# A middle norm summed with GpSimd's help, a router taken by quarters of the rows, a dense pass written out, and expert loads issued at the merge

## The chip, the cores and the metric

One NeuronCore of a Trainium2 chip runs the whole program. The time is device microseconds (us) of one execution; the median of several is given. Engines: TensorE (PE in the profile, PEld its weight loads), VectorE (DVE), ScalarE (ACT), GpSimd (POOL) and SyncE (SP), which here only issues DMAs.

## The reference

The program is a two-layer encoder trunk on 256 tokens of 1024 float32 channels. Per layer:

```
h = rmsnorm(x, g_mix[l]);  p = h @ w_in[l]
merged = gated sum of three branches (FoX attention, sparse attention, RWKV-7)
x = x + merged @ w_out[l]
h = rmsnorm(x, g_ffn[l])                      # the middle norm
layer 0: x = x + (silu(h @ w_gate) * (h @ w_up)) @ w_down          # d_ff 2816
layer 1: logits = h @ router_w + router_b; top 2 of 8, softmax -> gates
         x = x + sum_e gates[e] * swiglu_e(h)                      # d_ff 3584
out = rmsnorm(x, g_final)
```

rmsnorm is `x * rsqrt(mean(x*x) + 1e-6) * g` over the 1024 channels of a token.

## The kernel before, in words

Channels lie on partitions: x and h are [128, 8, 256], eight slices k of 128 channels by 256 tokens. Everything is float32; the profile records each full matmul as two. Each engine has its own instruction stream, written out by hand in program order, and waits on named semaphores (`need`, `wait_ge`). `open_bank`/`close_bank` take the 8 PSUM banks in turn on TensorE, `take`/`done` read and release one on another engine, `need_sb` waits until a bank has been read out.

**Weights.** SP issues all loads in program order. The mixers and the dense pass stream weights through three 2 MB slots in turn; the memory of slots 3 to 7 holds the mixer's tensors meanwhile (gates among them). The expert stage uses all eight as a ring, load n in slot n modulo 8, each load waiting for `slots_used`. A slot's next load waits for the bank that its last user closed (`before`, `released`). Ahead of the dense loop (L1211 to L1216) SP waits for all three slots, then issues gate, up and down loads; ahead of the experts it waits until all four output products have been added to x (L1241).

**End of a mixer (L847 to L877).** TensorE computes `pr0..3` (L856); VectorE multiplies by the gates and adds (L2000 to L2006, semaphore `merged`, 4 a layer). Then four output products `xo0..3` (L869), each 16 matmuls of 256 columns. VectorE adds each to x (L2010), ScalarE squares that pair of slices (L1414, `squares`), TensorE sums the squares over partitions with a matrix of ones, two matmuls a pair (L371), a pair behind each later product and the last after the fourth. ScalarE loads the table of the square root (L1416), takes it (L1426); VectorE takes the reciprocal (L1668) and makes the eight slices of h (L1671, `h_ready`).

**Dense pass (L888 to L923).** Five passes of 512 hidden channels run in a hardware loop and a last one of 256 follows: 32 gate matmuls, 32 up matmuls, 32 down matmuls per pass (L385, L909), the down products accumulating in banks 4 to 7. Four matmuls with zeros (L918) start these banks ahead of the loop, so that the loop never has to; TensorE then waits for all of h.

**Router (L932 to L967).** TensorE waits for all of h, makes the logits of each 128 tokens with 8 matmuls of 8 columns and one for the bias (L938, L939), then 16 transposes of h (L948) that ScalarE evacuates to ht, tokens on partitions. VectorE finds the top two (L2040 to L2060), ScalarE exponentiates (L1605), TensorE counts tokens per expert (L953 to L957) and spreads the table of items (L961, L962), VectorE makes the one-hot selections (L2110 to L2128). Then the first gather (L984) collects an item's tokens.

**Expert loop (L1004 to L1084).** One turn per item of up to 96 tokens: gate and up (L1030), down (L1047), the next gather, and the scatter of the item before (L994). It runs eight turns here.

GpSimd builds masks at the start, makes `Lo` (L1376) and copies in the mixer, and after layer 1 clears Ys and SpT (L1391 to L1394).

## Time and profile before

| | us |
|---|---|
| median of three runs | 1888.19 |
| lowest, highest | 1883.44, 1894.51 |
| the profiled execution | 1888.6 |
| its span in the trace | 1886.9 |
| busy: TensorE / VectorE / ScalarE / GpSimd | 1811.0 / 392.7 / 234.1 / 44.6 |

The span runs from the first instruction to the last in the trace; the execution's own time is 1.7 us longer. "Chain" below is the chain of work that ended last, followed back from the end: at each step to what released it. A piece "x64" of full matmuls is 32 of them. A window gives engine busy times, the clock granted to TensorE as a share of full speed, the share of time that the DMA engines were busy, and GB/s.

### The profile page before, as it was taken

Reading aid. Unit: us, or ns where it says so; the run is one execution under the profiler, and the core shown is the slowest. Engines: PE = TensorE matmul, PEld = TensorE weight load, DVE = VectorE, ACT = ScalarE, POOL = GpSimd, SP = SyncE. Lnnn points to the kernel's source line nnn. Section 1 sums busy time; section 2 is a strip of 40 time slices with the busy share of each in tenths; the row PEclk is TensorE's granted clock in tenths of the full one; section 3 lists DMA queues with packets and bytes.
Section 4 is the critical chain, followed back from the end, with each engine's and each line's share of the span. In section 5 each row is a group of like instructions: output and inputs, shape, how many; then the busy total and the mean of one; then the engine's idle time right before and its main releaser. Section 6 shows DMA issues by size and latency. Waiting matters only on the chain.

```text
span 1886.9 us, 42790 instructions
## 1 busy us (share of the span) xinstructions
PE 1811.0 (96%) x19764; PEld 1165.7 (62%) x19764; DVE 392.7 (21%) x807; ACT 234.1 (12%) x460; POOL 44.6 (2%) x102
## 2 busy tenths in 40 slices
PE   6999999999999999999799999999999999999996
PEld 5787878788887778878535444353443534445344
DVE  1256233100001456133310101101010010101102
ACT  1324120100001324111100000000000000000001
POOL 3000200000000000100000000000000000000000
PEclk9999999999999999989799999999999999999998
DMA  6432212543434332212899999999999999999970
GB/s 189 156 134 90 92 52 84 190 166 133 174 102 140 112 134 90 92 46 90 334 342 375 393 383 401 372 381 389 370 415 370 386 376 378 414 378 383 369 294 24
DMA packets 122842, 462.13 MB, mean 245 GB/s; under 512 B 9567, under 2 KB 20497, under 8 KB 106289
## 3 DMA queue, kind: packets, MB, share of 16 engines
q1 hardware_dynamic: 122672, 459.46, 64.0%
q8 instruction: 157, 2.57, 0.5%
q14 instruction: 13, 0.10, 0.0%
HBM read 458.39 MB, written 1.05 MB: 243 GB/s over the span
## 4 chain that ended last, share of the span: by engine, by line
PE 95%; DVE 2%; ACT 1%; issue 1%; SPq 0%; DMA 0%; DVEq 0%; ACTq 0%
PE bank L1030 31%; PE bank L385 26%; PE bank L1047 15%; PE bank L909 4%; PE bank L869 3%; PE bank L730 2%; PE bank L856 1%; PE bank L984 1%; PE bank L994 1%; PE bank L692 1%; PE bank L424 1%; PE bank L371 1%; PE bank L379 1%; PE bank L783 0%; PE bank L661 0%
## 5 line engine op out<-in xcount | busy, mean ns | idle before, releaser
L1030 PE MATMUL bank<-slot,xg 128*32 128x512 f32 (+1 forms) x6144 | 581.9, 539 | 0.0
L385 PE MATMUL bank<-h,slot 128*128 128x256 f32 x2176 | 488.0, 384 | 8.0 <-ACT rel L1478 5.3
L385 PEld LDWEIGHTS bank<-h,slot 128*128 128x128 f32 x2176 | 415.1, 192 | 70.5 <-issue 14.2
L1030 PEld LDWEIGHTS bank<-slot,xg 128*32 128x32 f32 x6144 | 198.9, 110 | 372.3 <-issue 369.0
L1047 PE MATMUL bank<-slot,aT 128*32 128x256 f32 x5376 | 293.0, 379 | 0.0
L1047 PEld LDWEIGHTS bank<-slot,aT 128*32 128x32 f32 x5376 | 174.9, 110 | 118.6 <-issue 6.2
L2154 DVE TENSOR_TENSOR av<-gs,bank 128x512 f32<-128x512 f32 (+1 forms) x48 | 29.8, 622 | 577.0 <-PE bank L1030 575.0
L909 PE MATMUL bank<-hid,slot 128*128 128x256 f32 x352 | 77.0, 380 | 0.9 <-DVE hid L2022 0.9
L909 PEld LDWEIGHTS bank<-hid,slot 128*128 128x128 f32 x352 | 66.9, 190 | 10.2 <-issue 1.2
L1622 ACT ACTIVATE gs<-bank 128x512 f32<-128x512 f32 (+1 forms) x48 | 25.2, 543 | 284.6 <-PE bank L1030 284.5
L869 PE MATMUL bank<-sq,slot 128*128 128x256 f32 x256 | 56.2, 379 | 0.0
L1627 ACT ACTIVATE SpT<-bank 128x512 f32<-128x512 f32 x8 | 4.8, 597 | 413.8 <-PE bank L1077 413.8
L869 PEld LDWEIGHTS bank<-sq,slot 128*128 128x128 f32 x256 | 48.7, 190 | 6.6
L2022 DVE TENSOR_TENSOR hid<-hsig,bank 128x512 f32<-128x512 f32 x11 | 7.6, 688 | 216.5 <-PE bank L385 216.5
L2142 DVE TENSOR_TENSOR x<-x,bank 128x512 f32<-128x512 f32 x36 | 22.4, 683 | 102.3 <-PE bank L994 102.3
L2170 DVE STREAM_TRANSPOSE xg<-bank 128x256 f32<-128x256 f32 x24 | 10.8, 450 | 136.0 <-PE bank L984 136.0
L1376 POOL TENSOR_TENSOR Lo<-Bm,level 128x512 f32<-128x512 f32 x16 | 21.1, 1334 | 722.4 <-DVE Bm L1893 678.9
L1507 ACT ACTIVATE gates<-bank,VB 128x256 f32<-128x256 f32 x48 | 20.1, 469 | 128.2 <-PE bank L385 128.1
L1622 ACT ACT_TABLE_LOAD x8 | 10.3, 1283 | 186.6 <-PE bank L1030 186.6
L984 PE MATMUL bank<-ht,Sl 128*32 128x256 f32 x432 | 26.9, 400 | 5.0 <-DVE Sl L2128 5.0
L2157 DVE STREAM_TRANSPOSE aT<-av 128x512 f32<-128x512 f32 (+1 forms) x48 | 30.9, 645 | 1.6
L994 PE MATMUL bank<-SpT,Ys 32*128 32x256 f32 x432 | 26.5, 383 | 1.8 <-DVE Ys L2172 1.0
(407 smaller groups left out, 1086.9 us busy)
## 6 DMA issues: line engine op xcount, KB each, us to landing
slot<-in_moe_w_gate SPq DMA_DIRECT2D x32, 2048.0 KB, 12.5
slot<-in_moe_w_up SPq DMA_DIRECT2D x32, 2048.0 KB, 17.9
slot<-in_moe_w_down SPq DMA_DIRECT2D x32, 2048.0 KB, 10.5
slot<-in_moe_w_gate SPq DMA_DIRECT2D x32, 1536.0 KB, 9.0
slot<-in_moe_w_up SPq DMA_DIRECT2D x32, 1536.0 KB, 11.1
slot<-in_moe_w_down SPq DMA_DIRECT2D x32, 1536.0 KB, 8.8
slot<-in_w_in SPq DMA_DIRECT2D x20, 2048.0 KB, 8.1
slot<-in_ffn_w_gate SPq DMA_DIRECT2D x5, 2048.0 KB, 7.8
```

The lines of the kernel that those rows point to most:

```text
L385: ins = mm(o, w[:, k, c:c + n], rhs[:, k, :], start=k == 0, stop=k == nk - 1)
L730: ins = mm(b[:, j, :], w[:, off + k, m * P:(m + 1) * P], src[:, k, :], start=k == 0, stop=k == nk - 1)
L869: ins = mm(b[:, j, :], w[:, k, 256 * g + P * j:256 * g + P * j + P], sq[:, k, :], start=k == 0, stop=k == KD - 1)
L909: ins = mm(v2(banks[4 + m // 2])[:, m % 2, :], w[:, k, m * P:(m + 1) * P], hid[:, k, :], start=first and k == 0, stop=last and k == nf - 1 ...
L984: ins = mm(banks[g][32 * p:32 * p + 32, 0:256].rearrange("s (b c) -> s b c", c=32), Sl[:, tt, 32 * g:32 * g + 32], strip(ht[:, tt, :], p), ...
L994: ins = mm(v2(banks[SCAT[p]])[:, j, :], Ys[32 * p:32 * p + 32, g, j * P:(j + 1) * P], SpT[32 * p:32 * p + 32, g, :], start=g == 0, stop=g ...
L1030: ins = mm(o.rearrange("s (b c) -> s b c", c=32), xg[:, g, k, :], strip(w[:, kk, :], p), start=k == 0, stop=k == KD - 1)
L1047: ins = mm(o[32 * p:32 * p + 32, :], aT[:, g, nb_ * q + b, :], w[:, b, 256 * p:256 * p + 256], start=half == 0 and q == 0 and b == 0 and g ...
L1622: A(gs[:, g, 0:width], banks[g][:, 0:width], ACT.Silu).then_inc(S["gs_done"], 1)
L2142: tt_(o, o, v2(banks[SCAT[p]]), ALU.add).then_inc(S["x_done"], 1)
L2154: tt_(av[:, g, 0:width], gs[:, g, 0:width], banks[3 + g][:, 0:width], ALU.mult).then_inc(S["av_done"], 1)
L2157: V.transpose(aT[:, g, 0:width // 32, :].rearrange("p b c -> p (b c)"), av[:, g, 0:width]).then_inc(S["aT_done"], 1)
```

## The change

Seven edits:

- *Sums.* In both layers GpSimd adds the squares of slices 2, 3 and then 4, 5 to those of slices 0, 1 (`added`). In layer 0 TensorE sums only slices 0, 1 and 6, 7, all after the fourth product.
- *Router by quarters (layer 1).* After each addition to x, VectorE multiplies two slices by the norm's weight alone into h (`xw_ready`). TensorE makes the logits and transposes of quarters 0 and 1 behind output products 1 and 2, and 2 and 3 behind the last. The sums of squares come out per token, in two columns of the logits' bank, from matmuls with one column of ones. ScalarE takes the root (`std_tok`), VectorE the reciprocal (`rs_tok`); the logits are scaled with it and the bias added on VectorE, and ht is scaled where ScalarE evacuates it.
- *Bias.* `b_rt` is loaded to 128 partitions.
- *First dense pass written out.* It starts banks 4 to 7 itself, and its first 8 matmuls wait slice by slice for h; the loop has four turns left. The zero matmuls are gone.
- *Dense loads.* Each of the first three waits for its own slot alone.
- *Expert loads.* The ring begins at slot 3 (`ring_at`). Loads 0 to 4 wait for layer 1's last `merged`, load 5 and later for the four additions to x, as before.
- A last wait for h counts one norm less, since layer 1's middle norm no longer makes h.

The diff, with unchanged lines and the list of semaphore names cut:

```diff
@@ -129,7 +129,8 @@
         w_rt = place("w_rt", [P, KD, NE])
-        b_rt = place("b_rt", [1, NE])
+        b_rt = place("b_rt", [P, NE])
+        rst = place("rst", [P, NT])
         x = place("x", [P, KD, T])
@@ -316,6 +317,9 @@
             released[name] = (bank_full[b], n)
+        def ring_at(n):
+            return (n + NS) % NSE
@@ -857,6 +861,37 @@
                 ssn = 2 * l + 1
+                tok = {}
+                def sums(ks):
+                    for tt in range(NT):
+                        for k in ks:
+                            ins = mm(tok["rt"][:, 2 * NE + tt:2 * NE + tt + 1], nsqs[1][:, k, tt * P:(tt + 1) * P],
+                                     ones[:, 0:1], start=False, stop=False, skip_group_check=True)
+                    return ins
+                def routed(g):
+                    need(pe, "xw_ready", g + 1)
+                    if g == 0:
+                        tok["rt"] = open_bank(pe, "rt")
+                    if g % 2 == 0:
+                        for tt in range(NT):
+                            tok[tt] = v4(open_bank(pe, f"ht{tt}{g // 2}"))
+                    ks = range(2 * g, 2 * g + 2)
+                    for tt in range(NT):
+                        for k in ks:
+                            mm(tok["rt"][:, tt * NE:(tt + 1) * NE], h[:, k, tt * P:(tt + 1) * P], w_rt[:, k, :],
+                               start=g == 0 and tt == 0 and k == 0, stop=False, skip_group_check=True)
+                    if g == 3:
+                        need(pe, "squares", 4 * ssn + g + 1)
+                        close_bank(sums(ks), "rt")
+                    for tt in range(NT):
+                        for k in ks:
+                            ins = nc.tensor.transpose(tok[tt][:, k % 4, :], h[:, k, tt * P:(tt + 1) * P], ident[:, :])
+                        if g % 2:
+                            close_bank(ins, f"ht{tt}{g // 2}")
                 for s in range(2):
@@ -869,12 +904,23 @@
                         close_bank(ins, n)
-                        if s == 0 and g == 1:
-                            ssb = open_bank(pe, f"ss{ssn}")
-                        if s or g:
-                            squares(ssb, ssn, 2 * s + g - 1, nsqs[l])
+                        if l and (s or g) and s + g < 2:
+                            routed(2 * s + g - 1)
                     free_slot(f"{l}wo{s}", f"{l}xo{2 * s + 1}")
-                close_bank(squares(ssb, ssn, 3, nsqs[l]), f"ss{ssn}")
+                if l:
+                    routed(2)
+                    need(pe, "added", 4)
+                    sums(range(2))
+                    routed(3)
+                else:
+                    b = open_bank(pe, f"ss{ssn}")
+                    need(pe, "added", 2 * (l + 1))
+                    for k in range(2):
+                        mm(b[:, 0:T], ones[:, :], nsqs[l][:, k, :], start=k == 0, stop=False)
+                    need(pe, "squares", 4 * ssn + 4)
+                    for k in range(KD - 2, KD):
+                        ins = mm(b[:, 0:T], ones[:, :], nsqs[l][:, k, :], start=False, stop=k == KD - 1)
+                    close_bank(ins, f"ss{ssn}")
@@ -897,7 +943,12 @@
                                 b = v2(banks[bi])
-                                unit(b[:, 0, :], w, 256 * g, P)
+                                if first and bi == 0:
+                                    for k in range(KD):
+                                        need(pe, "h_ready", KD + k + 1)
+                                        mm(b[:, 0, :], w[:, k, 0:P], h[:, k, :], start=k == 0, stop=k == KD - 1)
+                                else:
+                                    unit(b[:, 0, :], w, 256 * g, P)
                                 unit(b[:, 1, :], w, 256 * g + P, P).then_inc(bank_full[bi], 1)
@@ -907,18 +958,17 @@
                                     ins = mm(v2(banks[4 + m // 2])[:, m % 2, :], w[:, k, m * P:(m + 1) * P],
-                                             hid[:, k, :], start=first and k == 0, stop=last and k == nf - 1,
+                                             hid[:, k, :], start=first and k == 0 and m % 2 == 0, stop=last and k == nf - 1,
                                              skip_group_check=True)
...
                                     ins.then_inc(S["down_part"], 1)
+                                if first and g == 0 and m % 2:
+                                    ins.then_inc(bank_full[4 + m // 2], 1)
                         ins.then_inc(S["down_done"], 1)
-                    for bi in range(4, 8):
-                        mm(banks[bi][:, :], cst[:, 0:1].broadcast_to([P, P]), cst[:, 0:1].broadcast_to([P, 512]),
-                           start=True, stop=False, skip_group_check=True).then_inc(bank_full[bi], 1)
-                    need(pe, "h_ready", KD * 2)
-                    with pe.Fori(0, DI) as i:
+                    dense(0, 4, True, False)
+                    with pe.Fori(1, DI) as i:
                         dense(i, 4, False, False)
@@ -928,25 +978,6 @@
-            l = 1
-            need(pe, "h_ready", KD * 4)
-            b = open_bank(pe, "rt")
-            br = b[:, 0:2 * NE].rearrange("p (t e) -> p t e", t=2)
-            for tt in range(NT):
-                for k in range(KD):
-                    mm(br[:, tt, :], h[:, k, tt * P:(tt + 1) * P], w_rt[:, k, :], start=k == 0, stop=False)
-                ins = mm(br[:, tt, :], ones[0:1, :], b_rt[:, :], start=False, stop=True)
-            close_bank(ins, "rt")
-            for tt in range(NT):
-                for g in range(2):
-                    n = f"ht{tt}{g}"
-                    b = v4(open_bank(pe, n))
-                    for j in range(4):
-                        k = 4 * g + j
-                        ins = nc.tensor.transpose(b[:, j, :], h[:, k, tt * P:(tt + 1) * P], ident[:, :])
-                    close_bank(ins, n)
@@ -1005,7 +1036,7 @@
                 def slot(n):
-                    si, r = n % NSE, n // NSE
+                    si, r = ring_at(n), n // NSE
                     pe.wait_ge(slot_full[si], i * 48 + 16 * (loads[si] + r + 1))
@@ -1094,7 +1125,7 @@
             ins.then_inc(S["y_item"], 1)
-            need(pe, "h_ready", KD * (n + 1))
+            need(pe, "h_ready", KD * n)
             for tt in range(NT):
@@ -1129,7 +1160,7 @@
             vec(1, 48, lk(a["vres_v0"]))
-            sp.dma_start(b_rt[:, :], a["router_b"]).then_inc(S["rows_in"], 16)
+            sp.dma_start(b_rt[:, :], a["router_b"].broadcast_to([P, NE])).then_inc(S["rows_in"], 16)
@@ -1211,13 +1242,16 @@
                     sl3 = [(st0 + s) % NS for s in range(3)]
-                    for si in sl3:
-                        sm, v = before[(si, ld[si])]
-                        sp.wait_ge(sm, v)
                     wg = a["ffn_w_gate"][0].rearrange("(k p) n -> p k n", p=P)
...
                     wd = a["ffn_w_down"][0].rearrange("(k p) n -> p k n", p=P)
-                    with sp.Fori(0, DI) as i:
+                    for si, t_, src in ((0, c3(slots[sl3[0]], KD, 512), wg[:, :, 0:512]),
+                                        (1, c3(slots[sl3[1]], KD, 512), wu[:, :, 0:512]),
+                                        (2, c3(slots[sl3[2]], 4, D), wd[:, 0:4, :])):
+                        sm, v = before[(sl3[si], ld[sl3[si]])]
+                        sp.wait_ge(sm, v)
+                        sp.dma_start(t_, src).then_inc(slot_full[sl3[si]], 16)
+                    with sp.Fori(1, DI) as i:
                         srcs = [wg[:, :, bass.ds(i * 512, 512)], wu[:, :, bass.ds(i * 512, 512)],
@@ -1238,8 +1272,6 @@
-            for g in range(4):
-                need_sb(sp, f"1xo{g}")
             mg = a["moe_w_gate"][0].rearrange("e (k p) n -> e p k n", p=P)
@@ -1253,15 +1285,20 @@
                             src = t_[bass.ds(e, 1), :, r0:r0 + nb_, :]
-                            dst = c3(slots[n % NSE], nb_, D)
+                            dst = c3(slots[ring_at(n)], nb_, D)
                         else:
                             src = t_[bass.ds(e, 1), :, 2 * q:2 * q + 2, c0:c0 + 4 * width]
-                            dst = c3(slots[n % NSE], 2, 4 * width)
+                            dst = c3(slots[ring_at(n)], 2, 4 * width)
                         free(n)
-                        sp.dma_start(dst, src.rearrange("o p k n -> (o p) k n")).then_inc(slot_full[n % NSE], 16)
+                        sp.dma_start(dst, src.rearrange("o p k n -> (o p) k n")).then_inc(slot_full[ring_at(n)], 16)
                         n += 1
+            need(sp, "merged", 8)
             def first_free(n):
+                if n == NSE - NS:
+                    for g in range(4):
+                        need_sb(sp, f"1xo{g}")
                 if n >= NSE:
@@ -1387,6 +1424,15 @@
                                           Tt[o, :, :]).then_inc(S["t_copied"], 1)
+                o = nsqs[l]
+                for g in range(1, 3):
+                    need(gp, "squares", 4 * (2 * l + 1) + g + 1)
+                    if g > 1:
+                        need(gp, "added", 2 * l + 1)
+                    nc.gpsimd.tensor_tensor(o[:, 0:2, :], o[:, 0:2, :], o[:, 2 * g:2 * g + 2, :],
+                                            ALU.add).then_inc(S["added"], 1)
+                need(gp, "added", 2 * l + 2)
@@ -1587,8 +1633,8 @@
                 norm_sq(2 * l + 1, nsqs[l], x_out)
-                norm_std(2 * l + 1)
                 if l == 0:
+                    norm_std(2 * l + 1)
                     fl, _, _ = loop_fill["d"]
@@ -1600,13 +1646,16 @@
+            b = take(act, "rt")
+            A(rst[:, :], b[:, 2 * NE:2 * NE + NT], ACT.Sqrt, bias=cst[:, 1:2]).then_inc(S["std_tok"], 1)
             need(act, "route", 1)
+            need(act, "rs_tok", 1)
             for tt in range(NT):
...
                 for g in range(2):
-                    evac(f"ht{tt}{g}", ht[:, tt, 512 * g:512 * g + 512])
+                    evac(f"ht{tt}{g}", ht[:, tt, 512 * g:512 * g + 512], scale=rst[:, tt:tt + 1])
             act.wait_ge(S["tab_ready"], 2)
@@ -2008,11 +2057,18 @@
                     done(tt_(o, o, b, ALU.add), f"{l}xo{g}")
+                    if l:
+                        need_sb(dve, f"{l}xo{g}")
+                        for k in range(2 * g, 2 * g + 2):
+                            ins = V.tensor_scalar(h[:, k, :], x[:, k, :], col(VA, 24 + k), None, ALU.mult)
+                            if k % 2 == 0:
+                                step(ins)
+                        ins.then_inc(S["xw_ready"], 1)
                 for g in range(4):
...
                 V.memset(cst[:, 6:7], 0.0).then_inc(S["x_ready"], 1)
-                norm(2 * l + 1, 16 + 8 * l)
                 if l == 0:
+                    norm(2 * l + 1, 16 + 8 * l)
                     fl, _, _ = loop_fill["d"]
@@ -2036,9 +2092,18 @@
+            need(dve, "std_tok", 1)
+            V.reciprocal(rst[:, :], rst[:, :]).then_inc(S["rs_tok"], 1)
+            need(dve, "rs_tok", 1)
             b = take(dve, "rt")
-            done(V.tensor_copy(lg[:, :, :], b[:, 0:2 * NE].rearrange("p (t e) -> p t e", t=2)), "rt")
+            for t in range(NT):
+                ins = V.scalar_tensor_tensor(out=lg[:, t, :], in0=b[:, t * NE:(t + 1) * NE], scalar=rst[:, t:t + 1],
+                                             in1=b_rt[:, :], op0=ALU.mult, op1=ALU.add)
+                if t == 0:
+                    step(ins)
+            done(ins, "rt")
             need_sb(dve, "rt")
+            sync()
             for t in range(NT):
...
             sync()
```

## Rows read from the trace of the kernel before

**Rows 1.** the page, part 1: busy time, share of the span, instructions

```profile
PE 1811.0 (96%) x19764; PEld 1165.7 (62%) x19764; DVE 392.7 (21%) x807; ACT 234.1 (12%) x460; POOL 44.6 (2%) x102
```

**Rows 2.** expert turn: us, busy PE, PEld, DVE, ACT, POOL, clock, DMA share, GB/s

```profile
1163.00:1278.00 115.00, 115.00 (x1554) 51.25 (x1546) 13.27 (x24) 5.80 (x10) 0.00 (x0) 1.00 0.98 384
```

**Rows 3.** the chain in order of time, end of layer 0's mixer (start, us, what)

```profile
320.26 0.86 PE bank L371 x4
...
328.03 0.86 PE bank L371 x4
...
337.21 1.25 ACT L1416
...
339.10 1.76 DVE rs L1668
```

**Rows 4.** the same chain, end of layer 1's mixer to the expert loop

```profile
887.88 0.86 PE bank L371 x4
...
896.51 6.92 PE bank L869 x32
...
911.81 3.58 PE bank L938 x16
...
919.95 3.29 PE bank L948 x16
...
923.36 0.22 PE bank L954 x2
...
924.29 0.17 DVE pos L2074
...
932.93 4.50 PE bank L984 x48
```

**Rows 5.** groups by line and shape, GpSimd and VectorE (busy us, mean ns | idle)

```profile
L1376 POOL TENSOR_TENSOR Lo<-Bm,level 128x512 f32<-128x512 f32 x16 | 21.1, 1334 | 722.4 <-DVE Bm L1893 678.9 <-PE bank L692 43.5
...
L1714 DVE TENSOR_SCALAR F<-F 128x256 f32<-128x256 f32 x2 | 0.6, 285 | 0.0
```

**Rows 6.** the chain over the whole span, its longest pieces

```profile
344.50 29.58 PE bank L385 x128
...
387.89 27.63 PE bank L385 x128
...
579.47 1.76 DVE rs L1668
581.89 5.16 PE bank L379 x16
...
787.20 1.51 issue
```

**Rows 7.** the timeline at both middle norms (start, us, engine, line, operation)

```profile
336.24 0.40 SPq L1225 DMA_DIRECT2D slot<-in_ffn_w_gate  x1
...
338.21 3.61 PE L918 MATMUL bank<-cst 128*128 128x512 f32 x8
...
904.23 2.09 SPq L1261 DMA_DIRECT2D slot<-in_moe_w_gate  x4
...
920.20 0.24 DVE L2043 MAX8 mr<-lg 128x8 f32<-128x8 f32 x2
...
922.17 0.18 DVE L2060 TENSOR_TENSOR sl<-sl,eqr 128x16 f32<-128x16 f32 x1
```

**Rows 8.** the page, part 6: DMA issues, us from issue to landing

```profile
slot<-in_ffn_w_gate SPq DMA_DIRECT2D x5, 2048.0 KB, 7.8
```

**Rows 9.** the same view and columns, router and transposes of layer 1

```profile
912.00:924.00 12.00, 12.00 (x61) 11.90 (x62) 2.84 (x19) 2.71 (x6) 0.00 (x0) 0.55 1.02 426
```

**Rows 10.** the timeline at the start

```profile
6.37 0.25 SPq L1132 DMA_DIRECT2D b_rt<-in_router_b  x1
...
8.31 0.45 PE L348 MATMUL bank<-ident,rows 126*128 126x126 f32 x1 [8.31 <-DMA b_rt<-in_router_b]
```

**Rows 11.** DMA issues in the first 40 us

```profile
xt<-in_x SPq DMA_DIRECT2D x1, 1024.0 KB, 5.1
```

More of the change, by code:

```diff
@@ L234, in trunk @@
             "consts", "rows_in", "x_in", "smallw_in", "vecs", "sq_ready", "std_ready", "h_ready",
-            "x_ready", "squares", "fox_z", "fox_e", "fox_l", "fox_F", "max_ready", "exp_ready", "p_ready",
+            "x_ready", "squares", "added", "fox_z", "fox_e", "fox_l", "fox_F", "max_ready", "exp_ready", "p_ready",
             "css", "cstd", "cn_ready", "sel_ready", "shift_ready", "k_ready", "tanh_ready", "masks", "amasks", "w_zero",
@@ L239, in trunk @@
             "rel_used", "hid_sig", "hid_ready", "gates_in", "hT_done", "route", "route_e", "route_x",
-            "route_g", "route_n", "route_c", "route_t", "sel_item",
+            "route_g", "route_n", "xw_ready", "std_tok", "rs_tok", "route_c", "route_t", "sel_item",
             "out_tok", "stored", "vector_step", "scalar_step", "pool_step",
```

## The prediction

> **What bounds the kernel now.** I read the page first. Its busy line [rows 1] gives TensorE 1811.0 of 1886.9 us, so a gain has to shorten TensorE's work or one of the few stretches in which it waits. The windows view settles the second half of the kernel: in one turn of the expert loop [rows 2] TensorE is busy 115.00 of 115.00 us at granted clock 1.00, the DMA engines are busy 0.98 of the time and move 384 GB/s. TensorE sets the pace there and the loads just keep up. So whatever lets the expert loop begin earlier moves the end one to one. The chain of waits, read around the two middle norms, shows where TensorE is not in control. After layer 0's mixer [rows 3] it goes from TensorE's sums through ScalarE's table load and VectorE's reciprocal, and the dense pass starts at 344.50. After layer 1's mixer [rows 4] it runs from 903.43 (the last output product's end, 896.51 + 6.92) to the first gather at 932.93: 29.5 us of norm, router and routing chain. The change edits exactly these two places.
>
> **Layer 0, sums of squares.** Before, each pair of squares is summed by two matmuls behind the next output product; a pair takes 0.86 us [rows 3]. Two pairs lie between output products (320.26 and a like one at 328.03), on the chain. GpSimd now folds pairs 1 and 2 into pair 0 and four matmuls are left, all after the last product. That takes 2 x 0.86 = 1.7 us off the chain. The adds cost nothing if GpSimd keeps up: a 128x512 two-input operation takes it 1334 ns [rows 5], and its second add can start when the third squares exist, some 1.4 us after the third product, with 6.9 us of the fourth product over it; then TensorE needs it. Without that cover each would cost its 1.3 us. Behind the last product the chain stays: squares, ScalarE's table load of 1.25 us at 337.21, root, reciprocal 1.76 us from 339.10 [rows 3]; TensorE's first two remaining matmuls fit in front of the last squares, and the other two, 0.86 us, end under the table load.
>
> **Layer 0, start of the dense pass.** From the reciprocal's end at 340.86 to the end of the first 64 matmuls (344.50 + 29.58 = 374.08 [rows 6]) it was 33.2 us. Two things held it: all eight slices of h, and the gate weights, whose load was issued at 336.24 [rows 7] and takes 7.8 us to land [rows 8], so 344.0. Now each of the three loads waits for its own slot, and the gate load goes out when the branch weights are free, some 28 us earlier: it is covered. Matmul k waits for slice k alone. The kernel does this already at layer 1's first product [rows 6]: reciprocal ends 579.47 + 1.76 = 581.23, the eight gated matmuls (two records each) start at 581.89 and take 5.16, not the 3.45 us of eight at full clock (27.63/64 = 0.432 each), so the clock dip is in it. By that pattern: 0.66 + 5.16 + 56 x 0.432 = 30.0 us, a gain of 3.2. The old first batch has its dip too: 29.58 against 27.63 for 64 matmuls. The four zeroing matmuls (0.59 us records from 338.21 [rows 7]) lay under VectorE's work and cost nothing; without them TensorE idles some 3.5 us before h instead of 2.7, after which the rows show a dip anyway. Bounds: no dip, 1.7 more; twice the old dip, 1.9 less. The Trainium skill (TensorE: Matmul & The Clock Gate, "The HAM clock gate") has it that the half clock is what an idle array returns to and that activity releases it, which speaks against taking the zeroing away; by it alone this gain would be about 1.3. The trace agrees so far as that a batch after 2.7 us of idling took 29.58 us, not 27.63. The written-out pass adds no work; its first down matmuls start the banks themselves. Layer 0 together: **4.9 us** (3.0 to 6.6).
>
> **Layer 1, router.** A quarter of the router is 4 matmuls of 8 columns and 4 transposes. At half clock the 8 matmuls from 911.81 took 3.58 us and the 16 transposes from 919.95 took 3.29 [rows 4], the clock being 0.55 in that stretch [rows 9]; at full clock I take half, 0.22 and 0.10 to 0.12 (the full-clock pair at 923.36 took 0.22 [rows 4]). So a quarter is 0.88 + 0.48 = 1.36 us. After the second output product (887.88 [rows 4]): quarter 0, product 6.91, quarter 1, product 6.92: the last product ends at 904.43, 1.0 later than before (two quarters in, two pairs of sums out). Then quarter 2 (1.36), four one-column sums (0.88), quarter 3's router (0.88), four more sums (0.88): logits closed at 908.4. The last slice comes in time: VectorE's add 0.70 and two scalings at 0.29 each [rows 5] end 1.3 us after the product, the last squares 1.4 after, both before TensorE's 2.2 us are over. The first three quarters' scalings lie under output products. GpSimd's second add is some 5 us early here too. Before, VectorE copied the logits in 0.2 us and began the maxima at 920.20 [rows 7]. Now a small root (about 0.2), reciprocal and two scale-and-adds of small tiles (0.17 and 0.36) stand between, so maxima begin at 909.3. Exp's table load (1.3 us, like the other) moves behind that root and ends about 910.0; exp is wanted some 2 us after the maxima, so it stays hidden, as do the four evacuations of h's transpose, done by 913. From 920.20 to the gather at 932.93 were 12.7 us. In them TensorE was still transposing until 923.24 although sl was ready at 922.35 (922.17 + 0.18) [rows 7]: 0.9 goes. But the five count matmuls from 923.24 ran in a short full-clock spell (1.05 us to 924.29 [rows 4]); with nothing before them they would run at half clock, 1.1 more. So the gather starts at 909.3 + 12.9 = 922.2 to 922.4: **10.5 us** earlier (8.5 to 11.6: the lower end has TensorE at half clock for about half of its 4 us of small matmuls, the upper one the count matmuls at full clock).
>
> **Early expert loads.** Five go out at the last merge, near 875.5, instead of 904.23 [rows 7]. Nothing is queued on SP behind the new wait but these loads; w_out's landed long before. I cost this at nothing, neither gain nor loss: TensorE never waited for an expert load, and at 426 GB/s [rows 9] a 2 MB load takes 4.9 us, so five have landed by 901 and three more, issued near 905, by 920, before the gather is done. Were the loads needed, the new start would have been the first to feel it.
>
> **Start.** The router bias goes to 128 partitions instead of one, and it is the last of the small loads that TensorE's first transpose waits for: issued at 6.37, released 8.31 [rows 10]. Bounds: nothing, and 3.2 us (the 1 MB load of x takes 5.1 to land [rows 11] against these 1.9). It is 4 KB, so near the low end: **0.7 us lost**, on the path.
>
> **Sum.** 4.9 + 10.5 - 0.7 = 14.7. The profiled execution is 1888.6 us (span 1886.9), 0.4 over the median of 1888.19; so 1888.2 - 14.7 = **1873.5**. About 0.5%, 9.4 us, is what a measurement of this kernel can tell from no change.
>
> **Rivals.** (a) *The clock takes the gain.* The small matmuls behind the last product (4.0 us) run wholly at half clock, +4.0; the quarter between products brings a dip like the old one, +1.9; the dense start a longer one, +1.7. Gain 7.1: 1881. For: TensorE was at half clock through 11 us of just such matmuls [rows 9]. Against: before these it had stood idle 6 us; now it comes from full-size products. Chance 0.14, three parts of it within 0.5%. (b) *The token-side chain is longer than I count* (root, reciprocal, bias, exp's table on the path, about 3 us, and the bias load at its bound, 2.5 more): gain 9.2: 1879. Chance 0.08, half within 0.5%. (c) *TensorE waits for instructions at loop turns*, and it is slower. Both loops sit at other places in a longer stream; the row at 787.20 [rows 6] is such a gap, 1.51 us with nothing to wait for. Place: the four dense and eight expert turns, the latter with the DMA engines full. It decides from 1.2 us a turn (12 turns against 14.7); at 1.5 times the row, 2.25 each, it is 27 us: 1900. Against: TensorE is busy 115.00 us of 115.00 over a stretch that holds a turn's end [rows 2]. The Trainium skill (Runtime: NRT & Kernel Launch, "Instruction fetch mechanics") says that a taken branch outside the blocks at hand has to fetch its target before going on; the trace of before shows no such wait at that turn. Chance 0.04. (d) *It does not do what it says*: the first two quarters are not fed in time and TensorE waits the 1.3 us from a product's end to its scaled slice at each of three quarters, 3.9 in all: gain 10.8, 1877. Each slice has a whole product, 6.9 us, over it; this is inside the forecast's range and chance.
>
> **Numbers.** My forecast has 0.74, nearly all above 0.5%. Faster 0.80, same 0.16, slower 0.04. The terms' bounds give gains of 8.3 to 18.2, so 1870 to 1880; the runs of before scatter from 1883.44 to 1894.51, so I add about 3 each side: 1867 to 1883. That takes in (a), (b), (d) and leaves out (c).
>
> **What would show it.** Right: the third and fourth output products of layer 0 back to back; dense start near 340 with eight matmuls in about 5 us; gather about 18 us after layer 1's last product, not 29.5; GpSimd's adds done several us before TensorE's sums; expert turns still without idle. Wrong: TensorE waiting on GpSimd or on scaled h, a half-clock stretch that begins before the last product ends, gaps at loop turns, the first transpose later than 10 us, or any wait for an expert slot.

## The result and the profile after

The changed kernel takes 1938.8 us (median of 4, 1934.88 to 1945.04) against 1886.53 (1883.44 to 1894.51): ratio 1.0278, 95% interval 1.025 to 1.0306. It is 2.8% slower. 1873.5 was predicted, in a range of 1867 to 1883. Time in brackets is the lowest and highest run, or behind a ratio its 95% interval; every run below was measured beside the kernel before, whose median was 1883.7 to 1887.2 in those batches.

The changed kernel's page, part 1 (busy time) and the shares of the chain:

```profile
PE 1823.3 (94%) x19744; PEld 1160.6 (60%) x19744; DVE 390.2 (20%) x808; ACT 234.2 (12%) x460; POOL 49.7 (3%) x106
...
PE 93%; issue 3%; DVE 2%; ACT 1%; SPq 0%; DMA 0%; DVEq 0%; ACTq 0%
```

TensorE's busy time rose by 12 us [rows 1] and its share of the longer span fell; 3% of the chain is "issue", time in which the engine waits for nothing that the profile shows. The waits of TensorE, longest in total first (us in total, times, longest):

```profile
PE bank L1061 <- issue: 44.2, 14, 5.1
PE bank L352 <- DMA b_rt<-in_router_b: 9.2, 1, 9.2
PE bank L696 <- issue: 6.1, 6, 1.6
```

Before, L1061 (then L1030, the expert loop's gate and up products) had no such wait at all; now it has 14, two for each of seven returns to the loop's head. The chain at layer 0, behind layer 1's mixer, and around the first two returns (start, us, what):

```profile
308.93 27.64 PE bank L904 x128
...
342.28 6.42 PE bank L949 x16
348.70 24.17 PE bank L389 x112
...
386.68 27.63 PE bank L389 x128
...
872.14 13.81 PE bank L904 x64
...
920.64 4.75 PE bank L1015 x48
925.39 10.30 PE bank L1061 x96
...
1037.56 2.77 PE bank L1015 x48
1040.81 4.54 issue
1045.36 4.47 PE bank L1061 x17
1050.63 10.61 PE bank L1061 x79
...
1163.11 2.77 PE bank L1015 x48
1166.36 4.59 issue
1170.95 3.74 PE bank L1061 x17
1174.69 1.53 issue
```

The first turn, entered from above, is as before: 10.30 us for the 96 matmul records of L1061 behind the gather at 920.64. The second, whose gather starts at 1037.56, begins with 4.54 us of nothing, then 17 records in 4.47 us, another gap of 0.8 (1.53 at the next return), then the other 79 records. The busy view by stretch shows the rest of the cost (us, busy PE, PEld, DVE, ACT, POOL, clock, DMA share, GB/s):

```profile
1041.00:1045.00 4.00, 0.00 (x0) 0.00 (x0) 0.11 (x1) 0.00 (x0) 0.00 (x0) 0.89 1.01 412
1045.00:1049.00 4.00, 3.65 (x17) 0.97 (x18) 0.00 (x0) 0.00 (x0) 0.00 (x0) 0.50 1.02 420
1049.00:1052.00 3.00, 2.20 (x9) 0.43 (x11) 0.00 (x0) 0.00 (x0) 0.00 (x0) 0.50 0.99 404
```

The idle stretch is followed by half clock (0.50; still 0.50 from 1052 to 1054, then 0.91 from 1054 to 1056), at which the first records of the turn run. From gather to gather (1037.56 to 1163.11) a turn is 125.55 us here. Over the seven turns that begin with a return the mean is 124.77 against 114.93 before: 7 x 9.84 = 68.9 us lost. The first gather itself comes at 920.64 instead of 932.93 [rows 4]: 12.3 us gained. The difference, 56.6, is the difference of the two spans to 0.2 us (1943.3 and 1886.9). (Up to the loop a single trace can't tell the gain closely: in the seven traces whose code ahead of the loop is the same, this one among them, the first gather starts between 913.42 and 922.00, while the piece from layer 1's first output product to the gather is 48.5 in six of them and 49.3 in one.) So most of what the change was costed for happened (12.3 of 14.7 us), and something else took more than five times as much.

At layer 0 the output products now start at 308.93 and all four run back to back in one piece of 27.64 us. The eight gated matmuls (342.28) take 6.42 us. From the first output product to the end of the dense pass's first 64 matmuls it is 348.70 + 24.17 - 308.93 = 63.9 us, against 67.6 before (306.45 to 374.08, the end in [rows 6]). Behind layer 1's last product, which ends at 902.34, in the timeline's order (start, us, engine, line):

```profile
895.61 1.27 POOL L1433 TENSOR_TENSOR nsq<-nsq 128x512 f32<-128x512 f32 x1 [6.92 <-ACT nsq L1460]
...
902.18 0.95 PE L884 MATMUL bank<-w_rt,h 128*128 128x8 f32 x8
...
903.10 0.62 DVE L2063 TENSOR_SCALAR h<-x,VA 128x256 f32<-128x256 f32 x2
...
903.46 0.95 PE L869 MATMUL bank<-ones,nsq 128*128 128x1 f32 x8
...
904.27 1.04 PE L884 MATMUL bank<-w_rt,h 128*128 128x8 f32 x8
...
907.12 0.24 DVE L2108 MAX8 mr<-lg 128x8 f32<-128x8 f32 x2
...
909.32 0.59 PE L984 MATMUL bank<-sl,upto 128*128 128x8 f32 x2 [2.63 <-DVE sl L2125]
...
911.66 0.17 DVE L2139 TENSOR_TENSOR pos<-bank,sl 128x16 f32<-128x16 f32 x1 [1.57 <-PE bank L988]
```

GpSimd's second add is done at 896.9, 6.6 us before TensorE's sums (L869) read it at 903.46. The last scaled slices (L2063) are there at 903.7, before the last router matmuls at 904.27. The maxima (L2108) begin 4.8 us after the last product, not 16.8.

### The profile page after: what moved, and what is told of

Its sections match the earlier page's. It is cut to its first block, busy times and chain, and to the rows that moved or that the text cites. A ratio compares the mean times of both kernels' runs of the same rounds, so it can differ in the third digit from the quotient of the medians.

```text
span 1943.3 us, 42748 instructions
## 1 busy us (share of the span) xinstructions
PE 1823.3 (94%) x19744; PEld 1160.6 (60%) x19744; DVE 390.2 (20%) x808; ACT 234.2 (12%) x460; POOL 49.7 (3%) x106
## 4 chain that ended last, share of the span: by engine, by line
PE 93%; issue 3%; DVE 2%; ACT 1%; SPq 0%; DMA 0%; DVEq 0%; ACTq 0%
PE bank L1061 31%; PE bank L389 25%; PE bank L1078 15%; PE bank L960 4%; PE bank L904 3%; PE bank L734 2%; PE bank L860 1%; PE bank L1015 1%; PE bank L1025 1%; PE bank L696 1%; PE bank L428 1%; PE bank L383 1%; PE bank L375 0%; PE bank L787 0%; PE bank L665 0%
## 5 line engine op out<-in xcount | busy, mean ns | idle before, releaser
L1061 PE MATMUL bank<-slot,xg 128*32 128x512 f32 (+1 forms) x6144 | 605.5, 552 | 44.2 <-issue 44.2
L389 PE MATMUL bank<-h,slot 128*128 128x256 f32 x2160 | 481.5, 382 | 5.3 <-ACT rel L1524 5.3
L1061 PEld LDWEIGHTS bank<-slot,xg 128*32 128x32 f32 x6144 | 204.2, 112 | 435.8 <-issue 434.3
L389 PEld LDWEIGHTS bank<-h,slot 128*128 128x128 f32 x2160 | 409.6, 191 | 68.1 <-issue 12.5
L960 PEld LDWEIGHTS bank<-hid,slot 128*128 128x128 f32 x352 | 66.8, 190 | 10.3 <-issue 1.2
L904 PEld LDWEIGHTS bank<-sq,slot 128*128 128x128 f32 x256 | 48.5, 190 | 6.5
L1671 ACT ACT_TABLE_LOAD x8 | 10.3, 1283 | 256.4 <-PE bank L1061 256.4
L860 PE MATMUL bank<-yT,slot 128*128 128x256 f32 x128 | 28.0, 379 | 0.0
```

The source lines that it names most:

```text
L389: ins = mm(o, w[:, k, c:c + n], rhs[:, k, :], start=k == 0, stop=k == nk - 1)
L860: ins = mm(b[:, j, :], w[:, k, m * P:(m + 1) * P], yT[:, k, :], start=k == 0, stop=k == 3)
L904: ins = mm(b[:, j, :], w[:, k, 256 * g + P * j:256 * g + P * j + P], sq[:, k, :], start=k == 0, stop=k == KD - 1)
L960: ins = mm(v2(banks[4 + m // 2])[:, m % 2, :], w[:, k, m * P:(m + 1) * P], hid[:, k, :], start=first and k == 0 and m % 2 == 0, stop=last ...
L1061: ins = mm(o.rearrange("s (b c) -> s b c", c=32), xg[:, g, k, :], strip(w[:, kk, :], p), start=k == 0, stop=k == KD - 1)
L1671: A(gs[:, g, 0:width], banks[g][:, 0:width], ACT.Silu).then_inc(S["gs_done"], 1)
```

## The experiments

**Placing the loop of the changed kernel.**

```diff
+            pe.addr_align(256, offset=125, max_nops=0)
             pe.br("item_loop")
```

> The kernel after, with one edit: the first instruction of TensorE's expert loop is placed at position 125 of a block of 256 instructions (my estimate of where it lies in the kernel before; in the changed kernel everything ahead of it has moved it on by 92 positions). If the place of the loop in the instruction stream makes the waits of 4.5 and 1.6 us at each turn (theory 1), they go: no idle at the turns, a turn of 114.9 us, the gather still at 920.6, the whole near 1873 us. If the early expert loads or a full load queue make them (theory 2), they stay: about 1939 us. If position 125 is not what before had but the theory holds, the waits change in length.

Measured: 1871.71 us (1867.03 to 1873.53), ratio to before 0.9931 (0.9909 to 0.9954). No wait at any return; the chain, second turn:

```profile
917.55 4.92 PE bank L1015 x48
...
1034.63 2.73 PE bank L1015 x48
1037.36 10.30 PE bank L1062 x96
```

The turn is 114.89 us and the 96 records take 10.30 again. One instruction that computes nothing is worth 67 us. Theory 1 is right for this kernel, and the DMA engines are as busy at this return (1.00 to 1.02 from 1036 to 1042) as at the bad one.

**The mirror: the kernel before, placed at 217** (same line, offset 217).

> The kernel before, with one edit: its expert loop's first instruction placed at position 217, my estimate of where the changed kernel has it. Theory 1 (place): each of seven returns to the loop's head costs 9 to 10 us more, so 1886.5 + 7 x 9.7 = about 1954 us. Theory 2 (early loads): nothing changes, 1886.5 us.

Measured: 1917.09 us (1914.31 to 1922.6), ratio 1.0178 (1.015 to 1.0206). An untouched kernel loses 33 us by place alone, about half of the 67 that I expected. The likely reason is that my estimate of the changed kernel's position was off by an instruction or two; no run places it at 218 to 220, so that is not shown. The second turn:

```profile
1052.24 2.55 PE bank L1031 x18
1054.79 2.41 issue
1057.20 8.78 PE bank L1031 x78
```

There is no wait at the branch, only the inner one, 2.41 us after 18 records. 18 matmuls with their weight loads are 36 instructions, and 256 - 217 = 39: TensorE runs to the end of the block that holds the loop's head and waits for the next. At 217 the branch is at the very end of its block (217 + 38 = 255); in the changed kernel, whose inner wait comes one record earlier, it would lie just behind a block's start (the wait after 17 records puts the head at 218 to 220).

**No early expert loads, nothing placed** (the ring begins at slot 0; all expert loads wait for the additions).

```diff
-            return (n + NS) % NSE
+            return n % NSE
-            need(sp, "merged", 8)
+            for g in range(4):
+                need_sb(sp, f"1xo{g}")
```

> The kernel after without its early expert loads: the ring begins at slot 0 again and all expert loads wait for layer 1's four additions. TensorE's stream has the same instructions at the same places. Theory 1 (place): the waits at the turns stay, within 1 us of 1939, which also tests my nothing for the early loads. Theory 2 (early loads): the waits go, 1873 us.

Measured: 1944.59 us (two runs), ratio 1.0324 (1.0292 to 1.0355), mean turn 125.2 us. The early loads don't make the waits. It is 5.8 us more than the changed kernel's 1938.8, where within 1 was expected, with intervals that overlap; two runs can't tell whether that is real, and the placed pair below shows no difference.

**The prefetch hint 144 instructions earlier** (`if q == 1` for `if q == 2` at the mark).

> The kernel after with TensorE's prefetch hint for the branch back 144 instructions earlier in the loop body, 399 ahead of the branch instead of 255. If the distance of the hint is what matters (theory 3), the 4.5 us wait at each turn goes, and perhaps the 1.6 us one, 1873 to 1895 us. If it is the place of the loop's branch and head in their blocks (theory 1), both waits stay and the time is 1939 us.

Measured: 1940.31 us, ratio 1.0301 (1.0278 to 1.0323), 14 waits of 45.0 us in all. The distance between hint and branch is not what counts. Theory 3 falls.

**Control: the kernel before placed at 125.**

> Control: the kernel before with its expert loop's head placed at position 125 too. If the place theory is right and before already lay in a harmless place, the same as before, 1884 us within 3, no wait at the turns. If placing alone made the other kernel faster, this one is faster than before by some us as well, and the gain of the edits is smaller by that.

Measured: 1886.47 us (10 runs) against 1885.68 (18 runs), ratio 1.001 (0.9995 to 1.0025), mean turn 114.95. Placing is worth nothing where the place was harmless, so the gain of the placed changed kernel belongs to the edits: 12.0 us by the medians beside each other (1883.71 and 1871.71), 13 by the ratio.

**Placed at 125, without the early loads.**

> The placed kernel (expert loop at 125) without its early expert loads. My prediction costs them at nothing: 1871.7 us within 2. A rival: the loads keep the first expert turn fed only because they start early, so 1875 to 1880 and TensorE idle at its first expert products.

Measured: 1871.16 us (1869.84 to 1872.32), ratio 0.993 (0.9909 to 0.9952), against 1871.71 with them. They are worth nothing that these runs can tell, as costed.

**The dense part as before, nothing placed.** The loop takes all passes again, with the zeroing matmuls, the wait for all of h and the old load order; router, sums and expert loads stay as changed.

```diff
-                    dense(0, 4, True, False)
-                    with pe.Fori(1, DI) as i:
+                    for bi in range(4, 8):
+                        mm(banks[bi][:, :], cst[:, 0:1].broadcast_to([P, P]), cst[:, 0:1].broadcast_to([P, 512]),
+                           start=True, stop=False, skip_group_check=True).then_inc(bank_full[bi], 1)
+                    need(pe, "h_ready", KD * 2)
+                    with pe.Fori(0, DI) as i:
```

> The kernel after with layer 0's dense part as before (all passes in the loop, four zeroing matmuls, a wait for all of h, loads behind three waits) and nothing placed. The expert loop's head then lies 115 positions earlier than in the changed kernel, near position 103 by my estimate. Place theory: no waits at the turns, 1871.7 plus the dense start's gain (3 us predicted; 2 by the two traces) = 1874 us. If something else in the changed kernel makes the waits (router quarters, GpSimd's adds, early loads), they stay: 1940 us.

Measured: 1872.62 us (1869.98 to 1878.2), ratio 0.9938 (0.992 to 0.9956). Taking one harmless pass out of the stream takes 66 us away without any alignment: the loop's head moves to 371 instructions earlier. A turn is 115.21 us, 0.3 more than the shortest, and TensorE's waits at L1057 are two, of 0.6 us in all. The chain at its dense pass:

```profile
307.79 27.64 PE bank L904 x128
...
344.11 27.89 PE bank L389 x128
372.00 13.81 PE bank L955 x64
```

From the first output product to the end of the first 64 matmuls it is 64.2 us, only 0.3 more than the 63.9 of the changed kernel (62.6 to 64.2 over the nine versions with the written-out pass and no zeroing): here the first batch runs at full clock (27.89 for 64), where the kernel before had 29.58 [rows 6].

**Placed at 230.**

> The kernel after with the expert loop's head at position 230: 26 instructions before a block boundary, and its branch back 13 instructions behind one. Place theory: the wait inside the loop's top comes after about 11 matmul records instead of 17 and is longer than 2.4 us, some 3 us; the wait at the branch shortens only a little from 4.5 us, since 13 instructions are about 1 us. Turn about 124 us, the whole 1930 to 1945 us. If the wait at the branch needs the branch right at the boundary, it is gone: about 1905 us.

Measured: 1944.83 us, ratio 1.0322 (1.0282 to 1.0362), mean turn 125.2. The second turn:

```profile
1033.28 2.77 PE bank L1015 x48
1036.54 3.63 issue
1040.17 3.39 PE bank L1062 x12
1043.55 2.14 issue
```

Both waits, the inner one after 12 records (24 instructions; 256 - 230 = 26).

**Placed at 190 and at 30.**

> The kernel after with the expert loop's head at 190: 66 instructions ahead of a block boundary, its branch back at 228. By the place theory, in its finer form: the block behind the loop's head arrives some 4.8 us after the head runs (2.6 us of work and 2.0 to 2.4 of waiting at head 217). 66 instructions are about 3.5 us, so a wait of 1.3 us at each turn; no wait at the branch, which is 228 instructions into its block: 1871.7 + 7 x 1.4 = 1881 us. If any place away from the exact boundary is free of waits, 1872.

> The kernel after with the expert loop's head at 30, its branch back then 68 instructions into a block. By the finer form: the branch's target is fetched only once TensorE is in the branch's block, and takes about 5 us; 68 instructions of the gather are 1.9 us, so 3 us of waiting at the branch, with a half-clock start behind it, and no wait at the head: 1895 to 1905 us. If only a branch in the first few instructions of a block waits, 1872.

Measured at 190: 1887.75 us (8 runs), ratio 1.0022 (1.0008 to 1.0036), mean turn 116.93. At 30: 1892.91 us (1892.71 to 1894.67), ratio 1.0048 (1.003 to 1.0066), mean turn 117.63. The returns:

```profile
1033.28 3.43 PE bank L1062 x31
1036.71 1.54 issue
1038.25 7.46 PE bank L1062 x65
```

```profile
1038.01 2.77 PE bank L1015 x48
1041.26 1.62 issue
1042.88 10.51 PE bank L1062 x96
```

At 190 only the inner wait is left, 1.54 us after 31 records (62 instructions of 66). At 30 only the one at the branch, 1.62 us in the chain (2.15 us of idling), shorter than the 3 expected. At 190, 1881 was expected, 1887.75 came, since a turn is 2.0 us longer and not 1.4, and TensorE waits once more behind the last turn (2.30 us ahead of L1025; 1.89 at 217 ahead of L994). At 30 a half-clock start was expected and none came: the clock stays at 1.00 behind these short waits, at 30, 190 and 217 alike. Together with 217 the sizes fit one account. The next block is there 4.97 us after the loop's head runs (3.43 + 1.54) at 190, and 4.96 (2.55 + 2.41) at 217: a fetch of about 5 us. The loop's head is there 4.1 us after TensorE has run into the branch's block at 30 (68 instructions of the gather, 1.9 us, + 2.15), about 4.5 at 230, and 5.0 in the changed kernel, where the branch would be the block's first or second instruction. At 125 both fetches are covered by work.

**Placed at 125, the hint taken out.**

```diff
-                    if q == 2:
-                        near_end = pe.mark_branch_hint_location()
-                pe.br_lt(item_reg, items, on_true="item_loop", on_false="item_end").branch_hint(near_end)
+                pe.br_lt(item_reg, items, on_true="item_loop", on_false="item_end")
```

> The placed kernel (expert loop at 125) with TensorE's prefetch hint for the branch taken out. If the hint is what brings the loop's head in at a good place, TensorE now waits at each of the seven turns about as it did at a bad place, 4 to 5 us plus a half-clock start, also at position 125: 1871.7 + 7 x 6 = 1915 us. If the hint does nothing and only the place counts, 1872 us.

Measured: 1931.99 us (1927.87 to 1933.31), ratio 1.0242 (1.0215 to 1.0269), mean turn 122.9. The second turn:

```profile
1039.07 2.77 PE bank L1015 x48
1042.33 4.46 issue
1046.79 13.37 PE bank L1062 x96
```

Without the hint the return waits 4.46 us at a good place too, and the 96 records take 13.37 us instead of 10.30, about 29 of them at half clock (3.07 us more at 0.107 each). That is 60 us in all, more than the 43 expected, because the half-clock start costs 3 us of each turn's 8. The hint works, if the branch lies far enough inside its block.

**The fetches themselves.** The DMA view has a row for the fetching of instructions (packets, MB, share of the DMA engines' time). In the changed kernel's page, and then for the idle stretch alone, 1040.4 to 1045.3:

```profile
q8 instruction: 164, 2.69, 0.6%
```

```profile
q8 instruction: 1, 0.02, 1.3%
```

A packet is 16.4 KB. Narrower windows place this one: it moves from 1042.50 to 1043.5, and there is no other from 1040.4 to 1048.2; the next moves from 1048.29, in front of the inner wait's end. The same reading for the second turn of each run, in us from the start of its gather (whose last matmul ends at 2.8):

| run | packet starts | wait ends |
|---|---|---|
| changed kernel, return | 4.94 | 7.80 |
| changed kernel, inner | 10.73 | 13.07 |
| 230, return | 4.07 | 6.89 |
| 230, inner | 10.05 | 12.41 |
| 30, return | 2.10 | 4.87 |
| 125 without hint, return | 4.97 | 7.72 |
| 190, inner | 5.14 | 7.69 |
| 217 (kernel before), inner | 5.07 | 7.69 |

Each of the eight waits ends 2.3 to 2.9 us after such a packet starts. At 125 with the hint a packet starts at -0.73 and the next at 5.09, and nothing waits. In the changed kernel the return's packet starts when it does without any hint (4.94 and 4.97, 2.2 us behind the gather): the hint gained nothing there. At 30 and 230 it starts 1.3 and 1.7 us after TensorE has run into the branch's block. So the waits are waits for instructions. That the hinted fetch begins only once TensorE is in the branch's block fits these four starts; it is a reading, since the packets don't say which block they carry.

**Placed at 125, with zeroing ahead of the written-out pass, and the bias loaded late.** Four matmuls with zeros stand in front of the dense pass again, and the bias is the last of the later small loads.

```diff
+                    for bi in range(4, 8):
+                        mm(banks[bi][:, :], cst[:, 0:1].broadcast_to([P, P]), cst[:, 0:1].broadcast_to([P, 512]),
+                           start=True, stop=False, skip_group_check=True)
                     dense(0, 4, True, False)
```

> The placed kernel (expert loop at 125) with two repairs. First, four matmuls with zeros stand again ahead of layer 0's written-out dense pass. If the clock falls there because TensorE idles longer than before (the eight gated matmuls took 5.4 to 6.7 us, 5.2 expected), they take about 4 us now, 2 us gained; if the dip has nothing to do with the zeroing, they stay at 5.4 to 6.7. Second, the bias load goes to the end of the small loads, so TensorE's first transpose starts at 8.3 again or earlier, not 9.2: 0.9 us gained. Together 1871.7 - 2.9 = 1869 us; without the clock effect 1871.

Measured: 1867.49 us (1863.55 to 1875.72), ratio 0.9916 (0.9895 to 0.9937): the fastest median of all, though its interval overlaps that of the placed kernel without them. The trace shows both parts. The start of TensorE's transposes of x (L362) and the dense pass:

```profile
9.11 3.62 PE bank L362 x16
...
337.39 3.69 PE bank L971 x8
341.07 3.45 PE bank L949 x16
344.53 24.17 PE bank L389 x112
```

The eight gated matmuls (341.07) take 3.45 us instead of 5.11 to 6.66 in the nine other versions with a written-out pass. The granted clock is 1.00 from 334 to 344.5 here; in the changed kernel it was 0.74 from 340 to 342, TensorE idle, and 0.50 from 342 to 347. The dip is the price of taking the zeroing away. But the zeroing (3.69 us from 337.39) now ends 34.7 us after the first output product starts, and without it the gated matmuls start 33.35 after (342.28 - 308.93), so 1.3 of the 1.7 to 3.2 us is given back. TensorE's transposes of x start at 9.11 instead of 9.92.

## Why the prediction was wrong

**The step that failed is rival (c).** I named its mechanism, place and row, and then gave it 0.04, priced at 2.25 us a turn, because "TensorE is busy 115.00 us of 115.00 over a stretch that holds a turn's end" [rows 2]. That row says that the loop's old place was harmless. It says nothing of the new place, and the change moves the loop by 92 positions. So the sum held nothing for waits for instructions, and the rival's price was too small by a factor of four: 9.84 us at each of seven returns, 68.9 in all. The 1.51 us gap [rows 6] that I priced by is one wait in straight code; a return at a bad place has two waits, 4.5 and 0.8 to 1.8, and the first brings half clock to the products behind it. The dense loop's three returns (the prediction counts twelve turns, which hold ten returns) cost nothing: the chain has its batches of 27.63 us at 428.12, 469.56 and 511.00 with no wait in front of them. The Trainium skill (Runtime: NRT & Kernel Launch, "Instruction fetch mechanics") has blocks of 256 instructions and a fetch at a taken branch whose target is not at hand. I wrote that the trace of before shows no such wait, and let a fact of one place speak against a rule about places. The runs agree with the rule, and with its 256: the inner wait stands at 24, 36 and 62 recorded instructions behind heads at 230, 217 and 190, where 26, 39 and 66 are left of a block. Of the positions tried 103 (estimated) to 125 were free or nearly so, and 30, 190, 217 and 230 cost 2 to 10 us a turn. They were chosen, not drawn, so they don't give the chance that would have been right; with nothing known of the position 0.04 was too low.

**Without it the sum held.** Placed, the changed kernel gains 12 to 13 us; 14.7 was the forecast. Its 1871.7 us is nearer to the 1873.5 forecast than that partly by luck: the kernel before took 1883.7 beside it, not the 1888.2 that the sum starts from.

- *Sums and start of the dense pass:* 4.9 predicted, 3.7 measured (63.9 against 67.6 us; 3.4 to 5.0 over the nine versions). The first part, two pairs of sums off the chain, came as costed; a kernel with it and the old dense pass has 64.2 us. The written-out pass adds 0.3 us (0 to 1.6 over the versions) instead of 3.2, because I sized its eight gated matmuls by the ones at layer 1 (5.16) and they took 6.42 (5.11 to 6.66 over the versions), and the old first batch's dip, 1.95 us in [rows 6], is gone without the written-out pass too, once the sums are out of the way (27.89). I had costed the zeroing matmuls at nothing and they were worth 1.7 to 3.2 us of clock, though 1.3 of it goes to their own length. The rule that the prediction quotes from the Trainium skill (TensorE: Matmul & The Clock Gate, "The HAM clock gate"), that half clock is what an idle array returns to, was nearer than my row: by it this gain was 1.3, and 2.0 was measured (3.7 less the 1.7 of the sums). The same eight matmuls behind zeroing take 3.45.
- *Router:* 10.5 predicted, 10.4 measured: 872.14 to 920.64 is 48.5 us, against 58.9 before (874.06 to 932.93). Its parts agree: router matmuls near full clock (0.95 and 1.04 us for four; eight took 3.58 before [rows 4]), the count matmuls at half clock from 909.32 to 911.66 (2.3 us, 2.2 predicted), transposes no longer in front of them.
- *GpSimd's adds and early loads:* nothing predicted, nothing measured.
- *Bias:* 0.7 lost predicted, 0.9 measured. TensorE's first transpose waits 9.2 us, against 8.31 [rows 10]; over all traces it is 9.1 to 9.8 with the wide bias and 8.3 to 8.6 in the kernel before.

**Rivals.** (a) was partly right, at the dense start and not behind layer 1's products, where the clock held until 907. (b) and (d) did not happen.

## What to carry to other kernels

A large loop on an engine has a place in its instruction stream, and every edit ahead of it moves that place. Measure a change with the loop's head pinned, or at two positions, before the difference is given to the edit. In the profile look at the chain behind each return to a loop's head for "issue", and at the first records there for half clock, and ask the DMA view whether an instruction packet moves in the wait. Here one inert alignment was worth 67 us, and the edits under study 12 to 13. Work that costs nothing on the chain, like four matmuls with zeros, may still be holding the clock.

## What was not expected of the hardware

- A loop of 3,111 instructions on TensorE with a prefetch hint returns without a wait if its head lies at 125 of 256, and with 2.0, 2.7, 4.4 and 10.3 us more a turn at 190, 30, 217 (in the kernel before) and 230. Without the hint it costs 8.0 us at 125.
- Half clock came on in the wait itself (0.89 as the mean of 1041 to 1045) and lasted through the next 9 us (0.50), in which the inner wait fell, so a wait of 4.5 us cost about 7. Waits of 1.5 to 2.4 us left the clock at 1.00.
- A wait for instructions ended 2.3 to 2.9 us after the instruction queue's 16.4 KB packet had started, though the packet itself moved in about 1.1 us.
- A 128x512 add takes GpSimd 1.26 us, a little less than the 1.33 us of its products [rows 5].
